# The last layer's attention in query blocks of 128 instead of 106, its key tiles on the same borders, and the first layer's value product split at column 212

## The reference

```python
q = (rms_norm(c_q, cq_g) @ w_uq).reshape(b_, t_, MLA_HEADS, QK_HEAD)
k_nope = (ckv @ w_uk).reshape(b_, t_, MLA_HEADS, QK_NOPE)
v = (ckv @ w_uv).reshape(b_, t_, MLA_HEADS, V_HEAD)
...
s = jnp.where(mask[None, None], s, jnp.float32(-1e30))
p = jax.nn.softmax(s, axis=-1)
...
return h[:, N_META:]
```

## Time and profile before

| what | value |
|---|---|
| median of three runs | 1718.37 us |
| profiled execution | 1717.03 us |
| its span, first to last instruction | 1715.2 us |
| granted TensorE clock over the span | 0.998 |
| busy: PE, PEld, POOL, DVE, ACT | 99%, 93%, 70%, 52%, 28% |
| matmuls, and as many weight loads | 11976 |
| a turn of the pair loop, first layer | 93.0 us |
| a turn of the pair loop, last layer | 91.1 us |

### The profile page before, as it was taken

One profiled execution on the slowest core, in us unless ns is written; L12 is line 12 of the kernel. 1 busy time (PEld: TensorE's weight loads), 2 busy tenths in 40 slices (PEclk: granted clock), 3 DMA queues, 4 the chain that ended last, 5 costly groups with the idle time before them and its releaser, 6 DMA issues.

```text
span 1715.2 us, 32297 instructions
## 1 busy us (share of the span) xinstructions
PE 1698.3 (99%) x11976; PEld 1593.6 (93%) x11976; DVE 892.2 (52%) x1279; ACT 484.9 (28%) x867; POOL 1203.0 (70%) x1365
## 2 busy tenths in 40 slices
PE   7999999999999999999999999999999999999999
PEld 7999999999999999999999999999998888888887
DVE  7966758485545452212358757584856455322221
ACT  4423333332322331101134333333324223311110
POOL 7764848485688777777765748484857898777773
PEclk9999999999999999999999999999999999999999
DMA  4431222122232232232432313121222222322233
GB/s 158 139 98 62 92 72 81 65 92 86 87 110 74 86 123 100 86 98 86 162 116 76 107 59 98 60 92 66 92 86 98 98 86 86 139 96 98 88 121 112
DMA packets 49408, 164.23 MB, mean 96 GB/s; under 512 B 6048, under 2 KB 7456, under 8 KB 49056
## 3 DMA queue, kind: packets, MB, share of 16 engines
q1 hardware_dynamic: 41328, 146.56, 25.8%
q10 hardware_dynamic: 8032, 17.03, 3.0%
HBM read 152.21 MB, written 10.81 MB: 95 GB/s over the span
## 4 chain that ended last, share of the span: by engine, by line
PE 97%; DVE 1%; ACT 0%; issue 0%; ACTq 0%; POOL 0%; DVEq 0%; POOLq 0%
PE slots L507 85%; PE slots L572 3%; PE slots L605 3%; PE slots L667 2%; PE slots L590 1%; PE slots L541 1%; PE slots L557 1%; PE slots L575 0%; ACT residual_or_merged L955 0%; DVE sc_acc L1393 0%; DVE sc_acc L1397 0%; DVE residual_or_merged L1347 0%; PE slots L550 0%; DVE r_bias L1337 0%; DVE norm_diag L1103 0%
## 5 line engine op out<-in xcount | busy, mean ns | idle before, releaser
L419 POOL TENSOR_TENSOR w_lo<-w_raw,w_hi 128x256 fp32r<-128x256 f32 x1004 | 838.3, 865 | 20.9
L414 POOL TENSOR_SCALAR w_hi<-w_raw 128x1024 fp32r<-128x1024 f32 x251 | 289.5, 1154 | 337.0 <-PE slots L507 329.9
L507 PE MATMUL slots<-h_hi,w_hi 128*128 128x264 f32 (+1 forms) x2112 | 521.3, 311 | 0.0
L507 PE MATMUL slots<-h_lo,w_hi 128*128 128x264 f32 (+1 forms) x2112 | 515.6, 308 | 0.0
L507 PE MATMUL slots<-h_hi,w_lo 128*128 128x264 f32 (+1 forms) x2112 | 514.7, 308 | 0.0
L507 PEld LDWEIGHTS slots<-h_hi,w_hi 128*128 128x128 f32 x2112 | 342.7, 188 | 19.7
L507 PEld LDWEIGHTS slots<-h_hi,w_lo 128*128 128x128 f32 x2112 | 341.7, 188 | 19.1
L507 PEld LDWEIGHTS slots<-h_lo,w_hi 128*128 128x128 f32 x2112 | 342.0, 188 | 17.8
L507 PE MATMUL slots<-branch_hi,w_hi 128*128 128x264 f32 (+1 forms) x576 | 144.0, 313 | 10.5 <-DVE branch_lo L1109 8.7
L507 PE MATMUL slots<-branch_lo,w_hi 128*128 128x264 f32 (+1 forms) x576 | 142.9, 312 | 0.0
L507 PE MATMUL slots<-branch_hi,w_lo 128*128 128x264 f32 (+1 forms) x576 | 142.5, 311 | 0.0
(11 more groups left out here) (236 smaller groups left out, 2860.6 us busy)
## 6 DMA issues: line engine op xcount, KB each, us to landing
w_raw<-w_units SPq DMA_DIRECT2D x251, 512.0 KB, 3.3
stream<-sc_acc ACTq DMA_DIRECT2D x16, 264.0 KB, 2.1
sc_back<-stream SPq DMA_DIRECT2D x2, 2112.0 KB, 8.0
x_old<-stream SPq DMA_DIRECT2D x16, 264.0 KB, 4.3
stream<-residual_or_merged ACTq DMA_DIRECT2D x16, 264.0 KB, 2.4
ab_raw<-w_units SPq DMA_DIRECT2D x8, 512.0 KB, 4.2
residual_or_merged<-xt ACTq DMA_DIRECT2D x4, 528.0 KB, 7.9
stream<-xt ACTq DMA_DIRECT2D x1, 2112.0 KB, 9.5
```

The costliest lines, as they stand in the source:

```text
L414: pool.tensor_scalar(hi, raw, 1.0, 1.0, ALU.mult, ALU.mult).then_inc(sem("hi_part"), 1)
L419: op = pool.tensor_tensor(lo[:, cols], raw[:, cols], hi[:, cols].bitcast(F32), ALU.subtract)
L507: mm = pe.matmul(out[:, a_, 0:t1 - t0], w(k), x(k)[:, t0:t1], start=(n == 0), stop=(n == 3 * ks - 1))
```

## The change

In the last layer the queries are the 512 kept ones in four blocks of 128, and the key tiles have the same borders: four of 128 from token 16 on, and the 16 meta tokens as a fifth. A head has four steps instead of five. Every step has a transpose for each of its key tiles and one for the meta tile. The queries and their latents become `kept_only`. The row buffers get 128 partitions. `FILLS` gets a second row for the last layer, and the items in ACT's and DVE's steps get new step numbers there. In the first layer the blocks stay, but `attend` writes its two banks as columns 0 to 212 and 212 to 528, and its gate on DVE becomes two instructions. The pair loop of the last layer isn't aligned any more.

```diff
-TOKS = [(t * TOK, min(TOK, T - t * TOK)) for t in range(NTOK)]
-PT_STEP = T - TOK
+AV_SPLIT = 2 * TOK
+TOKS = ([(t * TOK, min(TOK, T - t * TOK)) for t in range(NTOK)], [(META + t * P, P) for t in range(4)] + [(0, META)])
+LANES = (TOK, P)
+STEPS = (NTOK, 4)
+PT_STEP = (T - TOK, T - META - P)
...
-FILLS = (8, 16, 4, 4, 4, 5, 5, 2, 6, 6, 7, 7, 6)
+FILLS = ((8, 16, 4, 4, 4, 5, 5, 2, 6, 6, 7, 7, 6), (8, 16, 5, 5, 6, 7, 3, 7, 8, 9, 6))
...
-                for j in range(i + 1):
-                    k0, nk = TOKS[j]
+                for j in [*range(i + 1)] + [4] * l:
+                    k0, nk = TOKS[l][j]
...
-                for j, (k0, nk) in enumerate(TOKS):
-                    for a_ in range(2):
-                        q0, q1 = max(k0, a_ * HALF), (a_ + 1) * HALF
+                for j, (k0, nk) in enumerate(TOKS[l]):
+                    for a_, (b0, q1) in enumerate(((0, AV_SPLIT), (AV_SPLIT, T)) if l == 0 else ((META, T),)):
+                        q0 = max(k0, b0)
...
-                    dense("CQ", l, 0, name, j, xg_hi, xg_lo, lambda k: at("xg_lo", l, 0, k + 1), False, ks)
+                    dense("CQ", l, 0, name, j, xg_hi, xg_lo, lambda k: at("xg_lo", l, 0, k + 1),
+                          l == DEPTH - 1 and name[0] == "q", ks)
...
-                with nc.Fori(0, PAIRS, engines=bass.OrderedEngineSet([pe.engine]), head_slot={pe.engine: 0}) as p:
+                with nc.Fori(0, PAIRS, engines=bass.OrderedEngineSet([pe.engine]), head_slot={pe.engine: 0} if l == 0 else None) as p:
...
-                                KQ).then_inc(sem("unit_used" if h else "att_mm"), 1)
+                                KQ, None, l == DEPTH - 1).then_inc(sem("unit_used" if h else "att_mm"), 1)
...
-                    for n in range(10):
-                        scores(l, p, n // 5, n % 5)
-                        fill(FILLS[n + 2])
-                        if n == 5:
+                    for n in range(2 * STEPS[l]):
+                        scores(l, p, n // STEPS[l], n % STEPS[l])
+                        fill(FILLS[l][n + 2])
+                        if n == STEPS[l]:
                             attend(l, p, 0)
...
-                    for n in range(10):
+                    for n in range(2 * STEPS[l]):
                         soften(n)
-                        if n == 4:
+                        if n == (4, 3)[l]:
                             gate(0)
-                        if n == 5:
+                        if n == STEPS[l]:
                             sc_copy(1)
...
                         if n == 1:
                             sc_gate(0)
-                        if n == 2:
+                        if n == (2, 1)[l]:
                             sc_out(0)
```

More of the change, by code:

```diff
@@ L163, in at @@
             stage, per = SIGNALS[name]
-            return sem(name), l * (STAGES[stage][0] * per) + i * per + (k + AHEAD.get(name, 0))
+            first, this = (per, per) if isinstance(per, int) else (per[0], per[l])
+            return sem(name), l * (STAGES[stage][0] * first) + i * this + (k + AHEAD.get(name, 0))
         def ready(stage, l, i, tile):
@@ L358, in _ @@
                     load("RG", l, i, 1)
-                    sp.wait_ge(*at("scores", l, PAIRS - 1, 10))
+                    sp.wait_ge(*at("scores", l, PAIRS - 1, 2 * STEPS[l]))
                     sp.wait_ge(*at("ab_split", l, i, 0))
@@ L466, in _ @@
                             pool.wait_ge(*at("q_summed", l, p, 1))
-                        pool.tensor_tensor(ct[h][rows], ct[h][rows], ct[6][rows], ALU.add).then_inc(
+                        pool.tensor_tensor(kept(l, ct[h][rows]), kept(l, ct[h][rows]), kept(l, ct[6][rows]), ALU.add).then_inc(
                             sem("q_summed"), 1)
@@ L534, in dense, with token_sums @@
                     mm.then_inc(sem("unit_used"), 1 + left * (j == per - 1))
-            def token_sums(out, groups):
-                for g_, t in [(g_, t) for g_ in range(len(groups)) for t in range(NTOK)]:
-                    t0, nt_ = TOKS[t]
+            def token_sums(l, out, groups, toks):
+                for g_, t in [(g_, t) for g_ in range(len(groups)) for t in range(toks)]:
+                    t0, nt_ = TOKS[l][t]
                     mm = pe.matmul(out[0:nt_, g_, t:t + 1], groups[g_][:, t0:t0 + nt_], ones[0:groups[g_].shape[0], 0:1],
@@ L543, in token_sums, with spread @@
                 return mm
-            def spread(out, diag, tile_there):
+            def spread(l, out, diag, tile_there):
                 pe.wait_ge(*tile_there(NTOK - 1))
                 for a_ in range(2):
-                    mm = pe.matmul(out[:, a_, 0:HALF], ones[0:TOK, :], diag[0:TOK, a_ * HALF:(a_ + 1) * HALF],
+                    mm = pe.matmul(out[:, a_, 0:HALF], ones[0:LANES[l], :], diag[0:LANES[l], a_ * HALF:(a_ + 1) * HALF],
                                    start=True, stop=True)
@@ L709, in fill @@
                                 mm.then_inc(sem("unit_used"), 1)
-                    fill(FILLS[0])
+                    fill(FILLS[l][0])
                     stat = free("ATT", l, p, "stat_q")
                     pe.wait_ge(*at("q_summed", l, p, 2))
-                    token_sums(stat, ct[0:2]).then_inc(sem("att_mm"), 1)
-                    fill(FILLS[1])
+                    token_sums(l, stat, ct[0:2], STEPS[l]).then_inc(sem("att_mm"), 1)
+                    fill(FILLS[l][1])
                     pe.wait_ge(*at("k_lo", l, p, 2))
@@ L720, in _ @@
                     pe.wait_ge(*was_read("ATT", l, p, "stat_q"))
-                    for n in range(10):
-                        scores(l, p, n // 5, n % 5)
-                        fill(FILLS[n + 2])
-                        if n == 5:
+                    for n in range(2 * STEPS[l]):
+                        scores(l, p, n // STEPS[l], n % STEPS[l])
+                        fill(FILLS[l][n + 2])
+                        if n == STEPS[l]:
                             attend(l, p, 0)
-                        turn(l, p, n // 5, n % 5)
-                    fill(FILLS[12])
+                        turn(l, p, n // STEPS[l], n % STEPS[l])
+                    fill(FILLS[l][-1])
                     attend(l, p, 1)
@@ L932, in _ @@
                         rows = slice(ROPE * h, ROPE * h + ROPE)
-                        act.activation(qr_both[rows, h, :], ct[7][rows], ACT.Copy).then_inc(sem("qr_hi"), 1)
-                    act.wait_ge(*at("q_ms", l, p, 3))
+                        act.activation(kept(l, qr_both[rows, h, :]), kept(l, ct[7][rows]), ACT.Copy).then_inc(sem("qr_hi"), 1)
+                    act.wait_ge(*at("q_ms", l, p, 3 if l == 0 else 1))
                     act.wait_ge(*was_read("ATT", l, p, "stat_q"))
-                    act.activation(q_ms[:], q_ms[:], ACT.Sqrt, bias=zero[0:TOK]).then_inc(sem("q_rms"), 1)
+                    act.activation(q_ms[:], q_ms[:], ACT.Sqrt, bias=zero).then_inc(sem("q_rms"), 1)
                     act.activation(token[:, 13:14], zero, ACT.Exp).then_inc(sem("table_exp"), 1)
@@ L977, in head_out @@
                         act.wait_ge(*was_read("ATT", l, p, f"av{h}"))
-                        act.activation(tile(y_hi, 2 * p + h), probs_out[h], ACT.Copy).then_inc(sem("att_hi"), 1)
+                        act.activation(kept(l, tile(y_hi, 2 * p + h)), kept(l, probs_out[h]), ACT.Copy).then_inc(sem("att_hi"), 1)
                     def sc_tanh(s):
@@ L1315, in _ @@
                         dve.wait_ge(*at("qr_hi", l, p, h + 1))
-                        lo_part(qr_both[other, h, :], ct[7][rows], qr_both[rows, h, :], "qr_lo")
+                        lo_part(kept(l, qr_both[other, h, :]), kept(l, ct[7][rows]), kept(l, qr_both[rows, h, :]), "qr_lo")
                     dve.wait_ge(*at("q_rms", l, p, 1))
@@ L1328, in row_bias @@
                     def row_bias(n):
-                        nq, keys = TOKS[n % 5][1], sum(TOKS[n % 5])
+                        q0, nq = TOKS[l][n % STEPS[l]]
+                        keys, c = q0 + nq, n // STEPS[l] * NTOK + n % STEPS[l]
                         dve.wait_ge(*at("scores", l, p, n + 1))
-                        whole = n % 5 < 4
+                        whole = keys < T
                         src = ps[0:nq, 2, 0, 0:keys] if whole else ps[0:nq, 2, :, 0:HALF]
```

245 lines of the change are left out of this document (130 added, 115 removed).

## The result

The changed kernel takes **1735.72 us** (median of 4 runs, 1734.15 to 1737.39), the kernel before, on the same chip, 1717.84 us (4 runs). The ratio is 1.0104, 95% interval 1.0089 to 1.0119: slower by 17.9 us. The forecast was 1718.6 us with a range up to 1725.0. It failed, on the slow side.

The account below looks back on a forecast made before the run. PE, busy 99% of the span, was taken as the bound: 1717.03 - 11.4 saved + 11.6 of slot waits = 1717.2 us profiled, 1718.6 us as median. The forecast's own range was 1715 to 1722, the overall range 1710.0 to 1725.0.

Parts of the forecast that it names:

- The two waits: Last layer's pairs: PE waits for slot 0 at ga0, 0.9 us, and slot 1 at x1, 2.0 us; 11.6 us in all.
- The clock: Rival, chance 0.15: PE's clock falls to half at the new standstills, at most 1.7 us each; 1722.0 to 1725.4 us.
- T + 3.95: Slot 0 comes free 3.95 us after T, the start of step 0's transposes; PE wants ga0 at T + 3.0.
- The entry: Entry into the last layer's pair loop: without the alignment's branch the loop follows in line, 2.2 us saved.
- Scores: Last layer's score matmuls: 3.89 us a head becomes 3.33; two masks fewer make 0.10 us a pair.
- Transposes: Last layer: 1.40 us a head becomes 1.37, so no change, with 65 ns assumed for each meta tile transpose.
- `attend`: Weights times values: 2.75 us a head becomes 2.61 in the last layer, 2.67 in the first; 1.7 us saved.
- Query columns: Products with queries as 512 columns: 180 in all, 12.1 ns less each, 2.2 us saved.
- The b0 wait: First fill behind step 0 waits for DVE's `sc_input(0)`: 0.1 us a pair won, 0.4 in all; none or 0.2 lost possible.
- The slots come free in time: Rival, chance 0.20 with "or mostly": no wait at ga0 or x1, 1707.0 us; with only one of them 1710.6 or 1715.0.
- the wider blocks save nothing: Rival, chance 0.06: 128-column loads don't hide behind 272 moving columns, the 4.9 us are gone; 1723.5 us.
- The loop's new place costs fetches: Rival, chance 0.07: the unaligned last-layer loop stops some 2.1 us in every turn; 1727.0 us.

Follow-up runs that it names:

- GpSimd idle: Changed kernel with GpSimd's split of the weights' low part cut to 256 of 1024 columns, last layer's attention units from the seventh on: 1729.5 us.
- a bias of one input: Changed kernel with VectorE's one-column row bias as a tensor_scalar with q_sc as scalar operand, not a second tensor: 1726.73 us.
- g0 early: Changed kernel with the drain of g0 in the last layer moved earlier, sc_gate in step 0: 1723.34 us.
- c1 early: Changed kernel with one filler product moved from step 4 to 3 and c1's copy put into step 3, last layer: 1718.63 us.
- both waits gone: Changed kernel with g0 drained earlier and c1 copied earlier in the last layer: 1708.79 us.
- the kernel before with c1 late: Kernel before, own blocks of 106, other last-layer fillers so that x1 follows c1 at once, ahead of attend: 1732.86 us.
- the loop without waits: Changed kernel with g0 drained and c1 copied earlier: 1708.79 us; with the one-input bias too, 1705.86 us.
- the unaligned kernel before: Kernel before with only the last layer's pair loop unaligned: 1713.33 us, ratio 0.998.

## Why the prediction was wrong, step by step

The path was right: PE's list, two new waits for a slot, the tiles and drains named. What failed in the sum is three sizes. The two waits were put at 11.6 us and measured 18.5. The clock was put at nothing, its fall being only a rival with a chance of 0.15, and cost 7.7. The work saved was put at 11.4 us and came to 5.8. These make 6.9, 7.7 and 5.6 us of the 20.2 us by which the profiled execution (1737.4) missed its forecast (1717.2).

- **Both waits: right in place and cause, wrong in size; these are the terms that failed first.** "0.9 us (0.7 to 1.1) a pair" measured 2.01, "2.0 us (1.6 to 2.3) a pair" measured 2.61. A tenth of the first is arithmetic: T + 3.95 and 0.1 later, less T + 3.0, is 1.0 and not 0.9. For the rest, the chain was built of durations read in steps where GpSimd happened to be idle, or at the end of an instruction, for the one-column bias; in the changed last layer GpSimd's instruction stood on top of it. With GpSimd idle 0.86 us were measured for the first, and with a bias of one input the two waits are 1.40 and 2.13 us. The kernel before had biases of 0.5 and 0.6 us at other steps of the same pair, each ending with GpSimd's instruction, and I read past them. Together 6.9 us of the miss.
- **The clock: the rival came true on top of the forecast.** Its chance of 0.15 was set with waits of 2.0 and 0.9. The rival's price, "at most half of its 3.4 us, 1.7" each, is right (1.54). Five stretches against one in the last layer, and a double one in the first, are five more: 7.7 us. The double one is none of the change's doing: the kernels with g0 early and with c1 early have the same first layer and a single one there. What the prediction held apart belongs together: the falls follow the waits, and with both waits gone none is left in the loop. Whether the 0.6 us that each wait had too little made the falls likelier is not shown: at x1, gaps of 2.26 us (bias with one input) were followed by a fall in three of four pairs, gaps of 2.74 in three of four or two of four. The rule of the Trainium skill (TensorE: Matmul & The Clock Gate, "A second HAM failure mode: psum-queue depth-cycling") that short idle spells between groups of matmuls pull PE to its low clock is borne out by the four of four in the kernel before with c1 late, though size alone doesn't decide: 2.25 us at ga0 alone lowered it in none of four pairs, 2.74 at x1 alone in two of four.
- **The entry: right number, partly by luck.** 2.2 us forecast, 2.2 found. The reason given, the branch, was right for the kernel before, but the changed kernel has the gain without the edit that was to bring it.
- **Scores: right in size.** 5 matmuls a step at 112, 128 and 183 ns for 144, 272 and 400 columns, by the median distances; 1.03 us less a pair where 1.12 were forecast, with the masks 0.06 instead of 0.10.
- **Transposes: "no change" was 0.3 us a pair too kind.** The thirty of 106 took 2.16 us and not 2.8, the new ones 2.46. The distance behind the last transpose of a step is only 28 ns (once, behind `attend` in the kernel before, 57), with 106, 104 or 16 weight columns alike, and the others stand at 88 to 94 ns with 106 and at 108 to 110 with 128. So the meta tile's 28 ns, for the 65 assumed, come from its being last and not from its short load. Five such places a head became four, and twenty others grew from some 91 to 109 ns.
- **`attend`: wrong sign in the last layer.** 2.61 us a head forecast, 2.83 measured, for 2.75 before. The trace before had no tile with so few rows, and I priced it by its columns without a bound above. That is 1.8 us of the miss. In the first layer 2.60 instead of 2.67: 0.6 us to the good.
- **Query columns:** 0.33 us a pair forecast; all products of a pair with the fills took 0.41 less. Right.
- **The b0 wait: wrong sign.** 0.1 a pair was to be won, 0.2 was lost, within the bounds given for it.
- **The other rivals.** "The slots come free in time" and "the wider blocks save nothing" are out, the latter since the loop without waits turns in 90.3 us for 91.1. "The loop's new place costs fetches" is out by the unaligned kernel before. None of the cases was the sum of two, the forecast's waits and the falls, which is what happened.

The miss in numbers, against the profiled executions: waits 18.5 for 11.6, the clock 7.7 for nothing. The spans differ by 1735.6 - 1715.2 = 20.4 us, so the savings came, by difference, to 18.5 + 7.7 - 20.4 = 5.8 us for 11.4. Some 1.5 us of small new waits (b0, and 0.17 us a pair ahead of the first scores) are lost in them.

## What to carry to other kernels

A wait read out of a chain must be priced with its neighbours at work: list every instance of each link, take the longest beside a busy GpSimd as the upper end, and look above all at instructions of one column that read two tensors. When a schedule is written by hand and a block is widened, look first at which small drain frees the next accumulation slot, since an order that is off by one step costs more here (about 26 us) than the wider blocks and what came with them bring (5 to 6 us). And where a change opens standstills like those here, 2.3 to 2.7 us on an otherwise full TensorE, add a fall of the clock behind each to the range.

## What the runs showed of the hardware that was not expected

- A one-column instruction of VectorE with two tensors in SBUF took 0.16 us with GpSimd idle and up to 0.96 us with it at work, ending within 0.02 us of GpSimd's instruction in the changed kernel's two waits; with a scalar operand in place of the second tensor 0.21 us.
- Standstills of 2.3 to 2.7 us at x1 were followed by 3.4 us at 1.2 GHz in most pairs (four of four, three of four, two of four, by kernel, in one execution each), which cost 1.54 us each; a standstill of 2.25 us some 18 us earlier in the pair, with none at x1, in none.
- The same branch ahead of the last layer's aligned loop took 3.37, 3.83 or 0.29 us in three kernels.
- Three matmuls of 16 rows and 512 columns between ones of 128 rows cost 1.02 us a head, where their columns come to 0.70.
- The instruction behind the last transpose of a step started 28 ns behind it, with 16, 104 or 106 weight columns alike.
